# Zeros for an expert scratch, written under the dense feed-forward instead of under the attention

## The reference

```python
x = x + mx[5] * _swiglu(_modulate(x, mx[3], mx[4]), ffn_w_gate[i], ffn_w_up[i], ffn_w_down[i])   # layer 0
...
def _swiglu(h, w_gate, w_up, w_down):
    return (jax.nn.silu(h @ w_gate) * (h @ w_up)) @ w_down
...
logits = (tok @ w_router).astype(jnp.float32)                                                    # layer 1
top_val, top_idx = lax.top_k(logits, TOP_K)
...
out = jax.ops.segment_sum(y, token_of, num_segments=n)
```

## Time and profile before

| | |
|---|---|
| median of 3 executions | 4548.6 us (4547.06 to 4548.66) |
| profiled execution, span | 4554.2 us |
| attention phase, within the span | 276.6 to about 571.7 us |
| dense feed-forward phase, within the span | about 746 to 1537 us |
| PE busy over the span | 3869.1 us (85%) |
| DVE / ACT / POOL busy | 2316.3 / 1755.4 / 829.9 us |
| DMA moved | 662.95 MB, mean 146 GB/s |

### The profile page before, as it was taken

One profiled execution on the slowest core, in us unless ns is written; L12 is line 12 of the kernel. 1 busy time (PEld: TensorE's weight loads), 2 busy tenths in 40 slices (PEclk: granted clock), 3 DMA queues, 4 the chain that ended last, 5 costly groups with the idle time before them and its releaser, 6 DMA issues. The chain is left out here.

```text
span 4554.2 us, 65309 instructions
## 1 busy us (share of the span) xinstructions
PE 3869.1 (85%) x23414; PEld 3520.6 (77%) x23415; DVE 2316.3 (51%) x3372; ACT 1755.4 (39%) x2324; POOL 829.9 (18%) x319
## 2 busy tenths in 40 slices
PE   5988867999999573869979979979699897997993
PEld 3964455777777452869979979978699897997993
DVE  2347733545545423756644444458444486454554
ACT  5146613322322132545433333345333354443442
POOL 0000000111111202322222112223222132221222
PEclk8988878999999786989989989999899998998996
DMA  4136634322322324655544444446443465444544
GB/s 166 34 131 222 222 105 171 102 92 92 108 95 65 140 113 98 225 174 185 184 129 133 138 137 135 134 154 229 138 154 132 135 221 178 157 138 137 175 166 178
DMA packets 433346, 662.95 MB, mean 146 GB/s; under 512 B 33361, under 2 KB 348881, under 8 KB 432977
## 3 DMA queue, kind: packets, MB, share of 16 engines
q1 hardware_dynamic: 413026, 587.84, 38.8%
q0 software_dynamic: 15776, 55.61, 3.4%
q10 hardware_dynamic: 4176, 15.21, 0.8%
HBM read 599.32 MB, written 59.29 MB: 145 GB/s over the span
## 5 line engine op out<-in xcount | busy, mean ns | idle before, releaser
L1822 POOL TENSOR_TENSOR moe_d_lo<-moe_raw_d,moe_d_hi 128x2048 fp32r<-128x2048 f32 x126 | 582.9, 4626 | 1947.3 <-ACT moe_d_hi L1962 1947.3
L2132 DVE SCALAR_TENSOR_TENSOR moe_y_t<-moe_y,moe_cols,moe_y_t 128x256 f32<-128x256 f32 (+3 forms) x936 | 480.7, 533 | 181.8 <-PE moe_y L1873 176.9
L1871 PE MATMUL moe_g<-moe_x,moe_g_hi 128*128 128x352 f32 (+3 forms) x1344 | 421.3, 313 | 145.0 <-issue 145.0
L2079 DVE TENSOR_TENSOR moe_g_lo<-moe_raw_g,moe_g_hi 128x2048 fp32r<-128x2048 f32 x127 | 359.2, 2829 | 214.2 <-ACT moe_g_hi L1962 212.9
L1872 PE MATMUL moe_g<-moe_x,moe_g_hi 128*128 128x352 f32 (+3 forms) x1344 | 421.0, 313 | 6.5 <-issue 6.5
L1873 PE MATMUL moe_g<-moe_x,moe_g_lo 128*128 128x352 f32 (+3 forms) x1344 | 420.1, 313 | 0.0
L1871 PE MATMUL moe_y<-moe_h,moe_d_hi 128*128 128x352 f32 (+3 forms) x1344 | 417.7, 311 | 1.3 <-DVE moe_y_t L2132 1.1
L1872 PE MATMUL moe_u<-moe_x,moe_u_hi 128*128 128x352 f32 (+3 forms) x1344 | 415.7, 309 | 0.0
L1872 PE MATMUL moe_y<-moe_h,moe_d_hi 128*128 128x352 f32 (+3 forms) x1344 | 415.7, 309 | 0.0
L1873 PE MATMUL moe_u<-moe_x,moe_u_lo 128*128 128x352 f32 (+3 forms) x1344 | 415.6, 309 | 0.0
L1873 PE MATMUL moe_y<-moe_h,moe_d_lo 128*128 128x352 f32 (+3 forms) x1344 | 415.5, 309 | 0.0
(11 more groups left out here) (317 smaller groups left out, 9509.7 us busy)
## 6 DMA issues: line engine op xcount, KB each, us to landing
moe_raw_g<-in_moe_w_gate SPq DMA_DIRECT2D x127, 1024.0 KB, 5.6
moe_raw_u<-in_moe_w_up SPq DMA_DIRECT2D x127, 1024.0 KB, 5.0
moe_raw_d<-in_moe_w_down SPq DMA_DIRECT2D x126, 1024.0 KB, 4.9
att_w_mod<-in_w_ada SPq DMA_DIRECT2D x20, 2048.0 KB, 8.6
scratch_y<-att_zeros SPq DMA_DIRECT2D x11, 2048.0 KB, 14.1
ffn_raw_g<-in_ffn_w_gate SPq DMA_DIRECT2D x22, 1024.0 KB, 5.5
ffn_raw_u<-in_ffn_w_up SPq DMA_DIRECT2D x22, 1024.0 KB, 5.4
ffn_raw_d<-in_ffn_w_down SPq DMA_DIRECT2D x22, 1024.0 KB, 4.9
```

The costliest lines, as they stand in the source:

```text
L1822: pool.tensor_tensor(d_lo[par][:, :, :], raw_d[:, :, :], d_hi[par][:, :, :].bitcast(F), ALU.subtract)\
L1871: pe.matmul(bank[:, 0:width], wh, moving[:, 0, 0:width], start=start, stop=False)
L2079: dve.tensor_tensor(lo[par][:, :, :], raw[:, :, :], hi[par][:, :, :].bitcast(F), ALU.subtract).then_inc(split, 1)
L2132: dve.scalar_tensor_tensor(y_t[:, db, 0:cols], y_ps[db % 4][:, 0:cols], gate, y_t[:, db, 0:cols], ALU.mult, ALU.add).then_inc(y_added, 1)
```

## The change

The attention no longer writes zeros: its tile, the POOL memset, the 11 writes and SP's waits for them are gone, and the 20 loads stand back to back. `expert_mlp_phase` has a new argument `to_clear`, given in the `ffn` call alone. There POOL sets a tile of 128x512 zeros ahead of its first fetch, and ACT, between `round_u(0, 0, 0)` and its first pass, issues 22 writes of 1 MB (half of the columns of a pass each, so 2 KB a row where it was 4 KB), and waits for them at the end of the phase.

```diff
 def attention_phase(nc, sink, w_ada, dram, keep):
...
-        zeros = sb("zeros", [P, D])
-        zeroed, cleared = sem("zeroed"), sem("cleared")
...
-            sp.wait_ge(zeroed, 1)
-            rows = dram["y"].rearrange("(a c p) d -> a p c d", p=P, c=TILES_PASS)
-            for i in range(max(len(REST_VECTORS), MAX_PASSES)):
-                if i < len(REST_VECTORS):
-                    load_mod(2 * i)
-                    load_mod(2 * i + 1)
-                if i < MAX_PASSES:
-
-                    sp.dma_start(rows[i], zeros[:, :].unsqueeze(1).to_broadcast([P, TILES_PASS, D])).then_inc(cleared, 16)
-            sp.wait_ge(cleared, 16 * MAX_PASSES)
-
-        @block.gpsimd
-        def _(pool):
-            pool.memset(zeros[:, :], 0.0).then_inc(zeroed, 1)
+            for i in range(len(REST_VECTORS)):
+                load_mod(2 * i)
+                load_mod(2 * i + 1)
...
+def expert_mlp_phase(nc, name, shape, weights, columns, ident, rows_of, y_rows, table, prepare=None, to_clear=None):
...
+        if to_clear is not None:
+            zeros = sb("zeros", [P, D // 2])
+            zeroed, cleared = sem("zeroed"), sem("cleared")
+            to_clear = to_clear.rearrange("(a c p) d -> a p c d", p=P, c=TILES_PASS)
...
         @block.gpsimd
         def _(pool):
             pool.sem_inc(x_turned, X0)
+            if to_clear is not None:
+                pool.memset(zeros[:, :], 0.0).then_inc(zeroed, 1)
...
             round_u(0, 0, 0)
             if table is not None:
                 ready_tokens(0)
+            if to_clear is not None:
+                act.wait_ge(zeroed, 1)
+                for a in range(MAX_PASSES):
+                    for half in range(2):
+                        act.dma_start(to_clear[a][:, :, half * D // 2:(half + 1) * D // 2],
+                                      zeros[:, :].unsqueeze(1).to_broadcast([P, TILES_PASS, D // 2])).then_inc(cleared, 16)
 
             each_pass(act, one_pass)
...
+            if to_clear is not None:
+                act.wait_ge(cleared, 32 * MAX_PASSES)
             act.sem_inc(all_stored, 1)
```

More of the change, by code:

```diff
@@ L1643, in _ @@
                 norm(t)
-def expert_mlp_phase(nc, name, shape, weights, columns, ident, rows_of, y_rows, table, prepare=None):
+def expert_mlp_phase(nc, name, shape, weights, columns, ident, rows_of, y_rows, table, prepare=None, to_clear=None):
     F, R = mybir.dt.float32, mybir.dt.float32r
@@ L2280, in backbone @@
         expert_mlp_phase(nc, "ffn", (SEQ // TOKENS, FF_DENSE // CHUNK_FF), (a["ffn_w_gate"], a["ffn_w_up"], a["ffn_w_down"]),
-                         keep["ffn_cols"], keep["ident"], token_tile, tile_rows(dram["y_dense"]), None)
+                         keep["ffn_cols"], keep["ident"], token_tile, tile_rows(dram["y_dense"]), None, None, dram["y"])
         pool_phase(nc, a["pool_w"], a["pool_scale"], keep["ident"], dram)
```

## The result

| | before | changed |
|---|---|---|
| median of the runs | 4548.6 us (4 runs, 4547.1 to 4554.4) | 4592.1 us (4 runs, 4585.6 to 4600.0) |
| profiled execution, span | 4554.2 us | 4591.5 us |
| ratio, 95% interval | | 1.0099 (1.0085 to 1.0113) |

The change costs 43.5 us by the medians (39 to 51 by the interval) and 37.3 us by the spans of the two profiled executions. That of the kernel before was a long one, 5.6 us over the median, and single executions scatter: timed again beside the experiments, the kernel before ran from 4533.0 to 4559.5 us. The traces account for about 38 us; what the medians say beyond that is within this scatter, and no trace shows a cause for it.

What follows compares the result with a forecast made beforehand. Engines' waits for one another were taken to bound the attention, PE the feed-forward. Terms 0 + 0.5 + 37.4 + 2.7 = +40.6 us on the 4548.6 us median gave 4589 us, range 4574 to 4616.

Steps and rivals of the forecast that it cites:

- step 1: Attention: 11 writes, the memset and two waits go, all beside the chain of DVE, ACT and PE; gain 0.
- step 2: Feed-forward start: POOL's memset stands ahead of the token rows' fetch, for which PE waits; +0.5 us.
- step 3: Feed-forward: ACT is held by its 22 issues until 19.9 MB of zeros and SP's 3.15 MB drain, to 829.5 us.
- short end of the range: Fast end of the forecast: more packets in flight, ACT's queue early by 1.9 us, no half clock; +30 us, 4579.
- step 6: Phase's end: ACT's waits for zeros cost 0; POOL's fetch for pass 1, sharing its DMA, costs 0.
- The limit, 99 packets an engine: Packets in flight on each DMA engine beyond which an issue holds its engine; between 99 and 172, taken as 99.
- step 4: Feed-forward: chunk 1's gate weights, rounded by ACT and split by DVE, come late; PE stands still 37.4 us.
- step 5: After the pause at chunk 1, PE runs 13 matmuls at half clock; +2.7 us.
- Rival A: Feed-forward: ACT is not held, its 22 issues take 7 to 12 us, hidden; 4549 us, chance 0.11.
- Rival B: Feed-forward: zeros drain slower than taken, as 2 KB rows in two queues at once; +61 us, 4609, chance 0.15.
- Rival C: Attention gets shorter with less traffic beside it; with ACT not held, 4540 us or less, chance 0.02.

Runs made afterwards that it cites:

- 8 writes: Of the changed kernel's 22 writes, 8 stay in ACT's burst and SP writes the rest in the attention: 4544.9 us, ratio 0.9993 to the kernel before.
- 14 (38.4 us, a gap): Of the changed kernel's 22 writes, 14 stay in ACT's burst and SP writes the rest in the attention: 4571.1 us, ratio 1.0054 to the kernel before.

## Why the prediction was right

- *The time.* 4589 us was forecast and 4592.1 measured; in spans, +40.6 us was forecast and +37.3 measured. Step by step some of the closeness is luck, since errors of up to 5 us cancelled.
- *The attention gives nothing* (step 1): right. The engines' waits and the phase's length are the same to 0.3 us, which is closer than the same attention agrees with itself (295.1 and 291.7 us, with all zeros in it).
- *The memset, +0.5 us* (step 2): wrong, it is 0. Its duration was right (0.52 us), but ahead of the fetch POOL had a wait to hide it in, which I did not look for.
- *ACT is held until 829.5 us* (step 3): right, 826.55, out of two errors. The queue came to the issues at 766.40, not 771.2: it runs ahead of the engine, with both roundings still to do. I had this as 1.9 us in the short end of the range; it was 4.8. And the drain took 60.2 us for my 58.3, because 0.96 MB of POOL's token rows for pass 1 went through the same DMA engines, which step 6 had at 0.
- *The limit, 99 packets an engine* (taken between 99 and 172): 106.
- *From there to PE 4.3 us* (step 4): it was 6.0. An activation table load of 1.28 us stands between, as it did before, where it was hidden; the order of ACT's instructions, shown with the change, has it ahead of the rounding, and I left it out. The gap: 38.0 us for 37.4. It fits so well by luck: the start 4.8 us early, the drain 1.9 us long, 1.7 us more on ACT's side, and chunk 0's end 1.9 us early.
- *Half clock, +2.7 us* (step 5): half right. 7 matmuls, not 13, ran slow, +1.5 us. In chunk 0 of the changed kernel the clock also rose sooner, behind the same pause of 9.5 us (0.75 over 771.1 to 777.0 us, for the 0.50 of the earlier trace rows); that gave 1.1 of the 1.9 us by which chunk 0 ended sooner, the phase having begun 0.8 us sooner. Why the clock rose sooner no run here shows.
- *The weight loads* (step 3): they shared the DMA engines and had slack. Chunk 1's gate weights landed at 784.0 us, and ACT had to begin on them by 794.4 - 4.3 = 790.1: 6 us. The trace before could have told this; I only assumed it.
- Rival A fell by the 22 issues themselves and by the burst on SP. Its threshold (ACT held for less than 20.9 us) agrees with 8 writes (18.5 us held, no gap) and 14 (38.4 us, a gap). Rival B fell: the mean rate over the hold was (19.73 + 3.15 + 0.96) MB / 60.15 us = 396 GB/s. Rival C fell by the times: none of the nine kernels is clearly faster than before, zeros in the attention or not.
- The rule of the Trainium skill ("DMA: Bandwidth & Descriptors", that the time to initiate a DMA is usually small beside the DMA) held here for one write a chunk, 0.55 us of 4.5, and for a single write; it did not for a burst, whose issues together take as long as the transfers.

What stays open: what exactly the queue counts (less an issue's own packets, 68 to 77 an engine were in flight at the end of each burst of ACT, but 95 and 107 in the two cases above), and why one issue in each burst of SP and ACT but the shortest took 7 to 12 us, two to three times its neighbours. In ACT's bursts it stands right behind one of 1.4 or 1.5 us that went in with more in flight than the others.

## What to carry to other kernels

A DMA issue is asynchronous only while its queue has room. Count the packets of a burst (here one for each contiguous row, and one that ends each transfer on each of the 16 engines). On SP and ACT, beyond some 100 an engine (85 with rows of 8 KB), the issuing engine was held at the rate of the DMA engines, about 2.6 us a MB, and everything behind the burst on that engine waited; POOL's queue took in some 460. Bulk writes belong on an engine with nothing urgent behind them, or one at a time between the engine's other work; there they cost nothing in these runs, and moving them from one free place to another gains nothing.

## What the runs showed of the hardware that I had not expected

- SP, ACT and POOL are all held by a burst: the median issue was 2.64 us on SP and 2.66 on ACT, and on POOL 15 issues of 0.75 us, 495 packets an engine, went in before a pause of 43.67 us. So POOL's queue is deeper (462 packets an engine in flight then), but not deep enough for 22.
- SP was also held when the burst was ACT's: its load of down weights in the changed kernel, with two loads ahead of it and the DMA engines shared, took 7.56 us to issue (0.41 before), and 11.98 and 20.11 us beside ACT's rows of 4 and 8 KB. In the changed kernel:

```profile
773.80 7.56 SPq L1782 DMA_DIRECT2D ffn_raw_d<-in_ffn_w_down  x1
```

- ACT's queue took up the DMA issues while two instructions of the engine ahead of them had not begun (766.40 us against 766.75 and 768.55). The wait between them, for POOL's memset, had long been met. A DMA that stands behind compute on its engine, with no unmet wait between, can so be issued before it.
